# The second half of a gate projection in two parts inside a later inversion, with three modulation blocks moved forward

## What is computed

```python
h = rmsnorm(x, norm_mix_g[0])
proj = h @ even_w_in[0]
y_a = rwkv7_group(...)                       # first branch, 8 heads of 64
y_b = gdn_group(proj[..., o_bq:o_bg],        # second branch: q, k, v
                proj[..., o_bg:o_bb],        # its gate: 256 x 512
                beta_logit, alpha_logit, ...)
mix = concatenate([y_a, y_b]) @ even_w_out[0]

def gdn_group(...):
    o = chunk_gated_delta_rule(q, k, v, beta, g)   # chunks of 64, a triangular solve in each
    return rmsnorm(o, norm_g) * silu(gate)

# second block, needed only much later:
mod_l = silu(c) @ w_ada[layer] + b_ada[layer]      # 6 * 1024 columns per layer
```

## Time and profile before

| | us |
|---|---|
| median of 3 runs | 1981.15 |
| lowest, highest | 1979.96, 1983.12 |
| profiled execution | 1984.14 |
| its span | 1982.3 |
| TensorE busy in the span | 1942.1 |
| VectorE busy | 1223.1 |
| ScalarE busy | 392.6 |

### The profile page before, as it was taken

The page is one execution under the profiler, slowest core; times in us unless marked ns, Lnnn a source line. Parts: engine busy times, 40 slices in busy tenths (PEclk is TensorE's granted clock), DMA queues, the critical chain, the costliest instruction groups (busy, mean ns, idle before and its releaser), DMA issues.

```text
span 1982.3 us, 26225 instructions
## 1 busy us (share of the span) xinstructions
PE 1942.1 (98%) x11406; PEld 1380.9 (70%) x11406; DVE 1223.1 (62%) x1727; ACT 392.6 (20%) x809; POOL 34.3 (2%) x65
## 2 busy tenths in 40 slices
PE   8999999999999999999999999999999999999998
PEld 7786669844675896448854548888874466669973
DVE  4555748785547687735435876555565574836776
ACT  2323020001214100041113722111100212421110
POOL 0000000000000000000000000000000000000000
PEclk8999999999999999999999999999999999999999
DMA  6435855654443656433151012222225443124442
GB/s 248 183 142 208 344 204 192 223 223 167 177 177 128 217 209 226 182 128 133 54 202 43 1 43 86 86 85 85 85 85 197 184 172 149 43 85 170 171 162 93
DMA packets 27491, 296.91 MB, mean 150 GB/s; under 512 B 3232, under 2 KB 3648, under 8 KB 10480
## 3 DMA queue, kind: packets, MB, share of 16 engines
q1 hardware_dynamic: 19728, 261.83, 35.2%
q0 software_dynamic: 7648, 33.40, 4.8%
HBM read 294.13 MB, written 1.08 MB: 149 GB/s over the span
## 4 chain that ended last, share of the span: by engine, by line
PE 90%; DVE 8%; ACT 1%; issue 1%; DMA 0%; SPq 0%; DVEq 0%; ACTq 0%
PE bank L358 88%; PE bank L721 1%; DVE small L890 1%; DVE arena L911 1%; PE bank L814 0%; DMA X<-in_x 0%; DVE arena L732 0%; DVE arena L517 0%; DVE arena L904 0%; DVE arena L675 0%; DVE arena L885 0%; DVE arena L1139 0%; ACT arena L848 0%; ACT arena L2566 0%; DVE arena L2712 0%
## 5 line engine op out<-in xcount | busy, mean ns | idle before, releaser
L358 PE MATMUL bank<-arena 64*64 64x64 f32 (+8 forms) x4612 | 656.0, 323 | 12.0 <-DVE arena L517 2.4
L358 PEld LDWEIGHTS bank<-arena 128*128 128x128 f32 (+3 forms) x4612 | 444.8, 168 | 203.5 <-issue 162.3
L358 PE MATMUL bank<-HT,ring 128*128 128x128 f32 (+1 forms) x2400 | 396.0, 324 | 5.0 <-ACT arena L652 2.1
L358 PEld LDWEIGHTS bank<-HT,ring 128*128 128x128 f32 x2400 | 352.2, 192 | 44.8 <-issue 12.0
L358 PE MATMUL bank<-ring,arena 128*128 128x512 f32 (+1 forms) x594 | 261.4, 593 | 0.6 <-ACT arena L730 0.6
L358 PEld LDWEIGHTS bank<-ring,arena 128*128 128x128 f32 (+1 forms) x594 | 111.5, 190 | 136.2 <-issue 135.8
L358 PE MATMUL bank<-ring,HT 128*128 128x512 f32 (+1 forms) x480 | 189.4, 552 | 1.0 <-ACT HT L2069 0.8
L358 PE MATMUL bank<-arena,ring 128*128 128x128 f32 (+4 forms) x1158 | 187.2, 322 | 0.0
L358 PEld LDWEIGHTS bank<-arena,ring 128*128 128x128 f32 (+3 forms) x1158 | 165.4, 189 | 15.1 <-issue 2.0
L358 PEld LDWEIGHTS bank<-ring,HT 128*128 128x128 f32 x480 | 85.4, 190 | 97.8 <-issue 94.6
L358 PE MATMUL bank<-HT,arena 128*128 128x128 f32 (+2 forms) x800 | 126.7, 322 | 0.0
(11 more groups left out here) (332 smaller groups left out, 1593.3 us busy)
## 6 DMA issues: line engine op xcount, KB each, us to landing
ring<-in_W SPq DMA_DIRECT2D x111, 2048.0 KB, 7.8
arena<-in_adaT POOLq DMA_DIRECT2D x36, 512.0 KB, 5.1
arena<-in_W SPq DMA_DIRECT2D x5, 2048.0 KB, 11.7
ring<-in_W SPq DMA_DIRECT2D x6, 1536.0 KB, 8.8
ring<-in_W SPq DMA_DIRECT2D x4, 1024.0 KB, 9.0
arena<-in_rel POOLq DMA_DIRECT2D x1, 2048.0 KB, 11.1
arena<-in_rpb POOLq DMA_DIRECT2D x1, 2048.0 KB, 9.3
arena<-gate_rows POOLq DMA_DIRECT2D x1, 2048.0 KB, 15.6
```

The lines of the kernel that those rows point to most:

```text
L358: return nc.tensor.matmul(out_, lhsT, rhs, start=start, stop=stop, skip_group_check=True)
```

## The change

The weight plan puts `bqkv0` ahead of block 1's weight. `slot_plan` keeps the weights of blocks 2 to 10 out of the slot that `bgate` has. The single held bank becomes a set, so that the bank of `gate b.1` can be held between its two parts. `pe_bgate` takes a range of the eight k tiles. Block 1 moves from ahead of `bqkv0` into step 1 of the first inversion, between `bqkv0`'s second half and `pe_scores("lak")`. In step 4 of that inversion block 2 stands where `pe_bgate(1)` was, and blocks 3, 4 and 5 each move up one place. Block 6 goes into `pe_bscores` ahead of the scores. In the second inversion step 1 ends with block 7, step 2 with the first part of `pe_bgate(1)` (k tiles 0 to 3), step 3 has blocks 8 and 9, and step 4 has the second part (k tiles 4 to 7) between LX and XLX; block 10 stays in step 5. ScalarE's Silu of the second gate tile moves behind its copy of LX 4 in the second inversion.

```diff
-    plan += ada[0:2] + [("bqkv0", 4096), ("bqkv1", 4096), ("bqkv2", 4096), ("bab", 256), ("bgate", 4096)] + ada[2:]
+    plan += ada[0:1] + [("bqkv0", 4096)] + ada[1:2] + [("bqkv1", 4096), ("bqkv2", 4096), ("bab", 256), ("bgate", 4096)] + ada[2:]
...
         allowed = list(range(RING)) + ([RING] if i in spare else [])
+        if names[i] in ADA[2:11]:
+            allowed.remove(slots[names.index("bgate")][0])
...
-                if state["bank"] % 8 == state["held"]:
+                while state["bank"] % 8 in state["held"]:
                     state["bank"] += 1
...
-        def pe_bgate(t):
+        def pe_bgate(t, ks=range(KT)):
             if t == 0:
-                state["block"] = weight("bgate").rearrange("p (k c) -> p k c", k=KT)
-            ps = open_bank(f"gate b.{t}")
-            for k in range(KT):
-                last = mm(ps[:, :], ht(k, t), state["block"][:, k, :], k == 0, k == KT - 1)
-            if t:
-                weight_used(last, "bgate")
-            else:
-                last.then_inc(tensor_done, pe.one())
-            pe.mark(f"gate b.{t}")
+                state["bgate"] = weight("bgate").rearrange("p (k c) -> p k c", k=KT)
+            if ks[0] == 0:
+                open_bank(f"gate b.{t}")
+                state["held"].add(banks[f"gate b.{t}"])
+            ps = PS[banks[f"gate b.{t}"]]
+            for k in ks:
+                last = mm(ps[:, :], ht(k, t), state["bgate"][:, k, :], k == 0, k == KT - 1)
+            if ks[-1] == KT - 1:
+                if t == 0:
+                    state["held"].remove(banks["gate b.0"])
+                if t:
+                    weight_used(last, "bgate")
+                else:
+                    last.then_inc(tensor_done, pe.one())
+                pe.mark(f"gate b.{t}")
...
                 pe_turn(f"vb{t}", [cv(8 + h)[:, t * P:(t + 1) * P] for h in range(4)])
+            pe_ada(6)
             for n, o in (("kkb", 4), ("qkb", 0)):
...
-            pe_ada(1)
             pe_half_block("bqkv0", "bq", 0, 0)
...
                     if k == 1:
+                        pe_ada(1)
                         pe_scores("lak", KF, KK)
...
                 elif k == 4:
-                    pe_bgate(1)
+                    pe_ada(2)
                     pe_bnorm_sum()
                 else:
-                    pe_ada(3)
+                    pe_ada(4)
                     pe_bnorm_spread()
...
                 elif k == 4:
-                    pe_ada(2)
-            pe_ada(4)
+                    pe_ada(3)
+            pe_ada(5)
...
                 pe_lx("gdn", k, 0, MASKED2, XI2)
                 if k < 4:
                     pe_chunk_in(k)
+                elif k == 4:
+                    pe_bgate(1, range(4, KT))
                 else:
-                    pe_ada(k + 5)
+                    pe_ada(10)
                 if k == 3:
-                    pe_ada(7)
+                    pe_ada(8)
                 pe_xlx("gdn", k, 0, LX2, XT2)
                 if k < 4:
                     pe_chunk_out(k)
-                    pe_ada((5, 6, 8)[k - 1])
+                if k in (1, 3):
+                    pe_ada(7 if k == 1 else 9)
+                elif k == 2:
+                    pe_bgate(1, range(4))
+            state["held"].remove(banks["gate b.1"])
             pe_ada(11)
...
+        def act_gate_b(t):
+            ps = full(act, f"gate b.{t}")
+            activation(GB[:, t, :], ps[:, :], ACT.Silu).then_inc(scalar_done, act.one())
+            act.mark(f"read gate b.{t}")
...
                 if k == 4:
-                    for t in range(2):
-                        ps = full(act, f"gate b.{t}")
-                        activation(GB[:, t, :], ps[:, :], ACT.Silu).then_inc(scalar_done, act.one())
-                        act.mark(f"read gate b.{t}")
+                    act_gate_b(0)
                     act.wait_ge(vector_done, at("conv5"))
...
             for k in range(1, 6):
                 act_lx("gdn", k, 0, LX2)
+                if k == 4:
+                    act_gate_b(1)
```

More of the change, by code:

```diff
@@ L315, in at @@
             return marks[name][1]
-        state = {"bank": 0, "last": [None] * 8, "w": 0, "held": None, "column": 0}
+        state = {"bank": 0, "last": [None] * 8, "w": 0, "held": set(), "column": 0}
         pe = Steps(nc.tensor, tensor_done, marks)
@@ L329, in open_bank @@
                 state["bank"] += 1
-            assert b != state["held"]
+            assert b not in state["held"]
             if state["last"][b]:
@@ L1078, in pe_ada @@
                 open_bank("ada")
-                state["held"] = banks["ada"]
+                state["held"].add(banks["ada"])
             ps = PS[banks["ada"]]
@@ L1087, in pe_ada @@
                 pe.mark("ada")
-                state["held"] = None
+                state["held"].remove(banks["ada"])
         def dve_ada_rows():
```

## The result

Measured beside each other, the kernel before takes 1982.98 us and the changed kernel 1986.85 us (median of 13 runs each), a ratio of 1.0021 with a 95% interval of 1.0014 to 1.0029: slower by 3.9 us. The kernel before stands 1.8 us above the median of its first three runs. The forecast was +1.8 us with a range up to 1986.5; the time lies above the range, and the shift is twice the one forecast.

A forecast was written before the change was run, and what follows sets the result against it. TensorE, busy 98% of the span, was taken to bound the kernel; -1.2 (filled stall) +3.0 (late weight) -1.35 +1.35 (clock) gave +1.8 us on the 1981.15 median, 1983.0 us, range 1978.8 to 1986.5.

The forecast's parts named there:

- edits 1 to 4: Block and gate moves in both inversions: no weight late, 1.23 us stall before the scores filled, `ub` 1.2 us earlier.
- Edit 5: Block 11's weight, planned into `bgate`'s slot: lands 9.7 us after issue, wanted after 6.0; wait costs 3.0 us.
- The second rival: Before block 11: weight lands within 6 us, no wait; 1978.5 to 1980.0 us; chance 12 in 100.
- the third: Rival before block 11: three 2 MB loads share engines, weight lands with the last; up to 1992.8 us; 13 in 100.
- The fourth: Rival before the second branch's scores: stall isn't filled, its 1.23 us stay; 1984.2 us; chance 5 in 100.
- loads in a row: Weights behind block 11's: landings 4.9 us apart, so block 12's lands at 231.7, wanted at 232.5, in time.
- the clock's term: Second inversion: old half-speed fall in step 1 gone (-1.35 us), new one behind block 11's wait (+1.35 us), together 0.
- the prediction's own sum: Whole change: -1.2 filled stall, +3.0 block 11's weight, -1.35 and +1.35 clock, giving +1.8 us.
- case of two falls: Second inversion: clock falls both at the old place and behind block 11's wait, weight landing at 9.7 us; +3.2 us.
- a pair of stalls: Stalls at 183.6 and 189.7 us, before scores and step 1, taken to cause the clock's fall; fall gone, 55 in 100.

The follow-up runs named there:

- the kernel with the centring moved: Changed kernel with block 11's weight in the slot block 8 leaves and VectorE's centring put ahead of grow 4: 1979.95 us, ratio 0.9985 to the kernel before.
- the first experiment's kernel: Changed kernel with block 11's weight also kept out of the gate weight's slot, in the one block 8 leaves: 1980.54 us, ratio 0.9991 to the kernel before.
- the old order with the late weight: Kernel before, order untouched, block 11's weight allowed only in block 9's slot: 1985.96 us, ratio 1.0017 to the kernel before.

## Why the prediction was wrong

*What was right.* The walk along the timeline held to some tenths: edits 1 to 4 came as worked out, with `u` at 169.16 (168.85 forecast, from a start 0.46 us later), the scores right behind block 6, the 1.09 and 0.88 us stalls kept, the second gate part's end at 216.34 (217.03 less the 1.35 us of a fall that did not come, and 0.46 later). Edit 5 named the term that decides, and its size: 10.0 us to landing against 9.7, a wait of 4.05 and 3.91 us against 3.7. The second rival (no wait) is excluded by both profiles of the changed kernel, and the third (three loads sharing the engines) by the landing of the first at 10.0 us. The fourth is excluded as well: the stall is filled, and taking block 6 out brings it back (+2.3 us with its clock). One reading beside them was off without harm: loads in a row were taken to land 4.9 us apart, and block 12's weight landed 6.4 us behind block 11's, in time by 0.7 us.

*The step that failed* is the clock's term, "At 1.35 us each they cancel": one fall gone against one new fall. The fall behind the 1.09 us stall was gone, and the new one behind the wait came in both profiles. But the new one was priced from step 1 in the earlier trace rows, and it cost 1.3 us in one profile and 2.4 us in the other. And the fall was looked for only where it had come before and behind the new wait: the stall of 1.58 us before the last chunks was passed over, from one execution in which nothing had happened there. The first profile of the changed kernel has a fall exactly there, worth 1.6 us. So the clock's term, forecast as 0, was +1.7 us in the first profile and +1.1 us in the second. The idle matmuls in the wait say nearly the same from the times: the clock costs 3.1 us in the changed kernel, less the 1.3 us of the fall that is gone, +1.8 us. With +1.7 in its place, and 3.4 us for the weight instead of 3.0, the prediction's own sum gives +3.9 us. Its case of two falls came to +3.2 us, but the two it meant were the old one and the new one, each at 1.35.

The reason given for the fall that went was not borne out either. It was called the effect of a pair of stalls, the first of which the change removes. Filling the first alone with idle matmuls left step 1 at 7.30 us; filling both brought it to 6.00. So a fall can come behind the 1.09 us stall alone, which the change keeps. Over all profiles that keep this stall, step 1 was slow in three of three with both stalls there, in one of one with idle matmuls in the first, and in one of seven with block 6 in the first. That the fall was gone in the changed kernel was as forecast; whether the first stall or block 6 in its place has a part in it stays open.

A second, smaller miss: the forecast was set on the median of three runs, 1981.15 us. Thirteen runs of the same kernel give 1982.98, so every absolute number was 1.8 us low, which alone brought the time from inside the range to just outside it.

## What to carry to other kernels

When work that reads a weight is moved later, its slot's next load moves with it: put the slot's release, the shortest landing seen for that size, and the next user's place side by side before anything else, and plan the tightest successor into another slot. A stall of TensorE that replaces several short ones costs its length and the clock behind it, here as much again. A fall of the clock seen, or not seen, in one profile is a coin that fell once: bound a clock term by every stall of that size in the stage, not by those where it happened to fall, and look at more than one execution before calling a stall harmless.

## What the runs showed of the hardware

Behind a long stall the clock always fell here, behind a short one it was a matter of place and of chance. In the thirteen profiles of this study, away from the span's two ends, the granted clock fell behind all six waits of 2.75 to 4.73 us, behind the 2.05 us stall between 520 and 535 us in 9 of 13 cases, behind the 1.58 us stall in 4 of 12 and behind the 1.09 us stall before step 1 in 5 of 11. But five other stalls, of 1.11 to 1.30 us, stand in every one of these profiles (at 75, 398, 774, 1141 and 1198 us in the kernel before), and behind none of these 65 did it fall:

```profile
1198.10 3.81 PE L358 MATMUL bank<-HT,ring 128*128 128x128 f32 x32 [1.30 <-DVE arena L2856]
```

So the length of a short stall does not tell whether the clock falls behind it; what sets these places apart was not tested. A fall cost 1.2 to 2.9 us, the last in the kernel with the centring moved, behind its 1.58 us stall (237.38 to 243.97 us, 6.59 us for what takes 3.74 at full clock). The same instructions with the same stalls fell in one execution and not in the next, so one profile shows only one draw.

Block 11's load landed 8.7 us after its issue at 205.46 in the first experiment's kernel and 8.8 at 215.91 in the old order with the late weight; beside GpSimd's row loads it was 10.0 and 9.9 us in the changed kernel's two profiles, 8.7 with these started later.
